# Scaled triangle rows of a state-space loop: sixteen GpSimd products against sixty-four ScalarE copies

## The chip, the cores and the metric

One core of a Trainium2 chip runs the whole program. Times are device microseconds (us) of an execution; the kernel before has a median of 1226.52 us over three runs (1224.99 to 1226.83). The trace belongs to one further execution, which took 1224.43 us, with a span of 1222.6 us from its first to its last instruction.

## The reference, cut to what matters

The network has two layers over 256 latent and 256 context tokens. The second one mixes attention with a state-space scan, run forwards and backwards over chunks of 128 tokens. Inside one chunk the scan needs, for each of 16 heads, a 128 x 128 matrix of decays:

```python
acs = jnp.cumsum(a.reshape(b, nc, Q, G, hg), axis=2)          # a = dt * A, Q = 128
lower = jnp.tril(jnp.ones((Q, Q), dtype=bool))[:, :, None, None]
seg = acs[:, :, :, None] - acs[:, :, None, :]
decay = jnp.exp(jnp.where(lower, seg, -jnp.inf))
cb = jnp.einsum('bcign,bcjgn->bcijg', Cm, Bm)
y = jnp.einsum('bcijgh,bcjghp->bcighp', cb[..., None] * decay, xdt)
...
y = y + jnp.einsum('bcign,bcghpn->bcighp', Cm, h_in) * jnp.exp(acs)[..., None]
```

The kernel gets seg from a matrix product. A triangle of ones (`before` or `after`) is multiplied with another triangle (`upto` or `from`) whose row k is scaled by a of token k. The scaled triangle is called rx. Its values for one head are 128 x 128; four heads lie beside each other in one slot of 128 x 512.

## The kernel before, in words

The program is written engine by engine, each engine with its own instruction stream, and semaphores order them. Nothing is scheduled automatically: an engine runs its instructions in written order and stops at the first wait that is not met.

Most of the time is matrix products of three parts each on TensorE (lines 1795 to 1797). Between the second layer's input projection and its attention stands the state-space stage, about 848 to 907 us in the trace. It ends in a loop of eight rounds k = 0 to 7 (`SEG`): four groups of four heads, two chunks each. A round has, in both directions d:

- **rx** (line 629, GpSimd): the scaled triangles of round k, two products of 128 x 512, in two of four slots. The slots of round k come free when the decay products of round k - 2 have read them (`seg_mm`).
- **decays(k)** (line 2266, TensorE): both directions' triangle products, summed in one of three PSUM banks `RB`. Each takes 128x512 of rx. Issued three rounds ahead: decays(k + 3) stands between the two other products of round k.
- **exp(k)** (line 968, ScalarE): the exponential of that bank, into `seg`.
- **mask products** (line 1605, VectorE): seg times the C-B products `CB`, one per direction. Both of its inputs lie in SBUF.
- **carried-state factors** (line 1611, VectorE): `CD` times `Cc`. The `CD` rows are broadcast into SBUF by DMAs that ScalarE issues (`rows_out`, line 939).
- **intra(k)** (line 2290, TensorE): the products within a chunk. **inter(k)** (line 2300, TensorE): the products with the carried state.
- Every second round also has `gate_y` on VectorE (lines 1594, 1596), `square_y` on ScalarE (line 959) and `sum_y` on TensorE (line 2274).

TensorE's order in round k is intra(k), decays(k + 3), inter(k), and then perhaps sum_y. ScalarE's order from round 1 to 5 is exp(k), a wait for inter(k - 1), two DMA issues, perhaps square_y, exp(k + 1). That wait is `act.wait_ge(s("inter_mm"), k)`.

Ahead of the loop VectorE scales the rows `XW` (line 1465), TensorE forms the chunk states from them (line 2256), ScalarE copies four of these out of PSUM (line 950), and VectorE joins them (1566, 1570).

Of the kernel before, what the change touches and what calls it, by code (L numbers as in the profile page):

```python
# [22 lines left out]
ALU = mybir.AluOpType  # L23
ACT = mybir.ActivationFunctionType
AX = mybir.AxisListType

P = 128
# [130 lines left out]
def build_trunk(nc, a, out):  # L158
    with ExitStack() as ctx:
        def sem(name):  # L160
            return ctx.enter_context(nc.semaphore(name))
# [16 lines left out]
        def view(name, shape, offset, dtype=F32):  # L178
            return nc.alloc_sbuf_tensor_at(name, [P] + list(shape), dtype, offset=offset)
# [72 lines left out]
        dts = view("dts", [8, TT * 32], r_misc + 24576)  # L252
# [38 lines left out]
        def cst(name, lo=0, hi=None, p0=0, p1=P):  # L291
            s, n = CONST_COLS[name]
            return const[p0:p1, s + lo:s + (n if hi is None else hi)]
# [14 lines left out]
        def s(name):  # L308
            if name not in S:
                S[name] = sem(name)  # L310
            return S[name]

        raw_loaded = [s(f"raw_loaded{i}") for i in range(RAW_SLOTS)]
        hi_split, lo_split, block_done = s("hi_split"), s("lo_split"), s("block_done")
# [23 lines left out]
        for n, (_, src, col) in enumerate(blocksA):  # L338
            stream.append(("w", src, 0, KD, col, BC))
            if 1 <= n <= 8:  # L340
                stream.append(("mod", 0, 1, n - 1))
# [33 lines left out]
        C_OUT = NW()  # L375
# [9 lines left out]
        rx = view("rx", [4, 512], r_split + idle)  # L385
# [37 lines left out]
        def _(sp):  # L423
# [15 lines left out]
            def load(r):  # L439
                item = stream[r]  # L440
                free(r)
                if item[0] == "mod":
                    _, l, j, k = item
                    if (l, j) == (1, 2):
                        rows_, cols_ = 2 * P * (k % 4), j * MOD_COLS + D * (k // 4)
                        sp.dma_start(raw_block(r, 2, D), tiles(a["mod_w"][l, rows_:rows_ + 2 * P, cols_:cols_ + D]))\
                            .then_inc(raw_loaded[r % RAW_SLOTS], 16)
                        return
                    sp.dma_start(raw[:, r % RAW_SLOTS, :],
                                 a["mod_w"][l, k * P:(k + 1) * P, j * MOD_COLS:(j + 1) * MOD_COLS])\  # L450
                        .then_inc(raw_loaded[r % RAW_SLOTS], 16)
                else:
                    _, src, k0, kt, col, cols = item
                    sp.dma_start(raw_block(r, kt, cols), src[:, k0:k0 + kt, col:col + cols])\
                        .then_inc(raw_loaded[r % RAW_SLOTS], 16)
# [146 lines left out]
        @block.gpsimd  # L602
        def _(pool):
            step = Chain(pool, s("pool_step"))

            nc.gpsimd.memset(U[:, :, :, :], 0.0).then_inc(s("pads_A"), 1)

            for f in range(KD):
                if f % 2:

                    pool.wait_ge(s("h_lo_dve"), f // 2 + 1)
                    nc.gpsimd.memset(ptap[:, f:f + 1], 0.0).then_inc(s("h_lo"), 1)
                    continue
                pool.wait_ge(s("h_hi"), f + 1)
                nc.gpsimd.tensor_tensor(Hlo[:, f, :], n_h[:, f % 4, :], Hhi[:, f, :].bitcast(F32), ALU.subtract)\  # L615
                    .then_inc(s("h_lo"), 1)

            pool.wait_ge(s("h_lo"), 3 * KD)
            nc.gpsimd.memset(XB[:, :, :, 0:2], 0.0).then_inc(s("pads_C"), 1)
            nc.gpsimd.memset(XB[:, :, :, 2 + LAT:4 + LAT], 0.0).then_inc(s("pads_C"), 1)  # L620
            pool.wait_ge(s("pads_C"), 2)
            pool.wait_ge(block_done, C_OUT)
            pool.wait_ge(s("da_ready"), 1)
            for k, (b, c) in enumerate(SEG):
                if k >= 2:
                    pool.wait_ge(s("seg_mm"), k - 1)
                for d in range(2):
                    at_ = 32 * c + 16 * d + 4 * b
                    nc.gpsimd.tensor_tensor(rx[:, (2 * k + d) % 4, :].rearrange("p (h i) -> p h i", h=4),
                                            cst(("upto", "from")[d]).unsqueeze(1).to_broadcast([P, 4, P]),  # L630
                                            dts[:, 7, at_:at_ + 4].unsqueeze(2).to_broadcast([P, 4, P]), ALU.mult)\
                        .then_inc(s("rx_ready"), 1)


        @block.scalar
        def _(act):
            step = Chain(act, s("act_step"))
            split = splitters(act, "hi")
            A = nc.scalar.activation
# [57 lines left out]
            for n, (kind, _, _) in enumerate(blocksA):  # L697
# [6 lines left out]
                if kind in ("k", "q"):  # L704
# [3 lines left out]
                    if nk == 0:  # L708
# [4 lines left out]
                      scale=vec[:, g0:g0 + 1]).then_inc(read_act, 1)  # L713
# [152 lines left out]
            for n, (kind, _, _) in enumerate(blocksC):  # L866
# [21 lines left out]
                if kind == "x":  # L888
# [3 lines left out]
                    if j < 5:  # L892
                        for i in range(2):
                            ins = A(XB[:, 2 * j + i, :, 2:2 + LAT], acc[:, lo + i, :].rearrange("p (s t) -> p s t", s=2),
                                    ACT.Copy)
# [40 lines left out]
            def rows_out(q):  # L936

                (b, c), d = SEG[q // 2], q % 2
                act.dma_start(CD[q % 6], row_store[2 * c + d, 4 * b:4 * b + 4, :].rearrange("h i -> (h i)")
                              .partition_broadcast(P)).then_inc(s(f"cd_loaded{q % 6}"), 16)  # L940

            act.wait_ge(s("qsc_copied"), 1)
            A(qsc[:, 0:LT, :], qsc[:, 0:LT, :], ACT.Sqrt, scale=1.0 / C_HD, bias=epsc[:, 0:1]).then_inc(s("qsc_root"), 1)
            act.wait_ge(s("row_stored"), 32)
            act.wait_ge(s("cb_mm"), 1)
            rows_out(0)
            rows_out(1)
            for k in range(4):
                act.wait_ge(s("xw_used"), (2, 2, 5, 5)[k])
                A(state[:, k // 2 * 2, k % 2, :], stbank[k // 2 * 4 + k % 2], ACT.Copy).then_inc(s("state_act"), 1)  # L950
            act.wait_ge(s("xw_used"), 6)

            def square_y(b):

                for f in (2 * b, 2 * b + 1):
                    act.wait_ge(s("yg_ready"), f + 1)
                    if f >= 2:
                        act.wait_ge(s("ssy_mm"), f - 1)
                    A(ysq[:, f % 2, :], XC[:, f, 0:LAT], ACT.Square).then_inc(s("ysq_ready"), 1)


            for q in range(2, 6):
                rows_out(q)
            for k in range(8):
                act.wait_ge(s("seg_mm"), k + 1)
                if k >= 2:
                    act.wait_ge(s("intra_mm"), k - 1)
                A(seg[:, (2 * k + 1) % 4, :], RB[k % 3][:, :], ACT.Exp).then_inc(s("decay_ready"), 1)
                if 1 <= k < 6:
                    act.wait_ge(s("inter_mm"), k)  # L970
                    for q in (2 * k + 4, 2 * k + 5):
                        rows_out(q)
                if k % 2 == 1 and k > 1:
                    square_y(k // 2 - 1)
# [1398 lines left out]
SEG = [(b, c) for b in range(4) for c in range(2)]  # L2373
# [58 lines left out]
```

## Time and profile before

| what | value |
|---|---|
| median of three runs | 1226.52 us (1224.99 to 1226.83) |
| the profiled execution, and its span | 1224.43 us, 1222.6 us |
| TensorE busy | 1163.7 us, 95% |
| VectorE busy | 715.9 us, 59% |
| ScalarE busy | 483.2 us, 40% |
| GpSimd busy | 30.2 us, 2%, 31 instructions |
| the chain that ended last | TensorE 77%, VectorE 17%, DMA 2%, ScalarE 2% |

The shares say that TensorE sets the time nearly everywhere. They are a mean over stages, so the state-space stage has to be read by itself: in the profile's 40 slices of 30.6 us, TensorE's digit is under 9 in the first two, in the last, and in the 29th and 30th (856 to 917 us), where the state-space loop runs. GpSimd's digit is 5 in the 29th slice, 1 in the 28th, 2 in the second, and 0 in all others.

### The profile page before, as it was taken

The numbers are of one execution on the slowest core, as the hardware profiler recorded it, in microseconds if no ns is written. First come the engines' busy times: TensorE is split into PE (matmuls) and PEld (weight loads), VectorE is DVE, ScalarE is ACT, GpSimd is POOL, SyncE is SP. The second block draws the span as 40 slices with busy tenths as digits, with TensorE's granted clock in tenths as the row PEclk, the third lists the DMA queues.
The fourth block names the chain that finished last, engine by engine and source line by source line (L and its number), as shares of the span: only waits on it lengthen the run. The fifth ranks groups of instructions, "written<-read, shape, count | busy, mean of one in ns | idle before, by whom it ended". The sixth has DMA issues, their size and how long they took to land.

```text
span 1222.6 us, 18071 instructions
## 1 busy us (share of the span) xinstructions
PE 1163.7 (95%) x7366; PEld 943.9 (77%) x7366; DVE 715.9 (59%) x1167; ACT 483.2 (40%) x720; POOL 30.2 (2%) x31
## 2 busy tenths in 40 slices
PE   4799999999999999999999999999889999999998
PEld 2477775677678888888887668898455798999998
DVE  2779997843543333423333378977979645556544
ACT  3413325652443332222222333464148735554432
POOL 0200000000000000000000000001500000000000
PEclk9799999999999999999999999999999999999999
DMA  8745436016553223333124553434214157646632
GB/s 323 285 138 175 161 138 215 2 61 214 174 172 103 86 58 98 126 115 103 57 67 151 191 192 109 131 115 147 84 37 139 36 173 254 194 132 215 203 111 96
DMA packets 123308, 170.70 MB, mean 140 GB/s; under 512 B 4797, under 2 KB 112743, under 8 KB 117991
## 3 DMA queue, kind: packets, MB, share of 16 engines
q1 hardware_dynamic: 120406, 164.99, 40.6%
q10 hardware_dynamic: 2833, 4.74, 1.2%
q8 instruction: 50, 0.82, 0.3%
q14 instruction: 19, 0.16, 0.0%
HBM read 168.63 MB, written 1.08 MB: 139 GB/s over the span
## 4 chain that ended last, share of the span: by engine, by line
PE 77%; DVE 17%; DMA 2%; ACT 2%; issue 2%; SPq 0%; POOL 0%; ACTq 0%; DVEq 0%
PE acc L1795 21%; PE acc L1796 20%; PE acc L1797 20%; DVE Y L1174 5%; PE pmod L1740 2%; DVE w_lo L544 2%; PE acc L1812 1%; PE acc L1814 1%; PE acc L1813 1%; PE p L1701 1%; PE acc L1701 1%; PE p L2347 1%; DVE seg L1605 1%; PE acc L2321 1%; DMA raw<-in_mod_w 1%
## 5 line engine op out<-in xcount | busy, mean ns | idle before, releaser
L544 DVE TENSOR_TENSOR w_lo<-raw,w_hi 128x1024 fp32r<-128x1024 f32 x234 | 259.6, 1151 | 242.0 <-ACT w_hi L535 241.7
L535 ACT ACTIVATE w_hi<-raw 128x1024 fp32r<-128x1024 f32 (+1 forms) x236 | 221.6, 987 | 438.4 <-PE acc L1797 408.0
L1795 PE MATMUL acc<-Hhi,w_hi 128*128 128x512 f32 (+1 forms) x992 | 339.7, 342 | 8.1 <-POOL Hlo L615 5.8
L1797 PE MATMUL acc<-Hhi,w_lo 128*128 128x512 f32 (+1 forms) x992 | 337.3, 340 | 0.0
L1796 PE MATMUL acc<-Hlo,w_hi 128*128 128x512 f32 (+1 forms) x992 | 337.2, 340 | 0.0
L1795 PEld LDWEIGHTS acc<-Hhi,w_hi 128*128 128x128 f32 x992 | 188.5, 190 | 33.6 <-issue 10.0
L1797 PEld LDWEIGHTS acc<-Hhi,w_lo 128*128 128x128 f32 x992 | 188.4, 190 | 20.9
L1796 PEld LDWEIGHTS acc<-Hlo,w_hi 128*128 128x128 f32 x992 | 188.6, 190 | 20.5
L1795 PE MATMUL acc<-hid_hi,w_hi 128*128 128x512 f32 (+1 forms) x448 | 157.1, 351 | 0.0
L1796 PE MATMUL acc<-hid_lo,w_hi 128*128 128x512 f32 (+1 forms) x448 | 155.7, 348 | 0.0
L1797 PE MATMUL acc<-hid_hi,w_lo 128*128 128x512 f32 (+1 forms) x448 | 155.7, 348 | 0.0
L1795 PEld LDWEIGHTS acc<-hid_hi,w_hi 128*128 128x128 f32 x448 | 84.8, 189 | 15.2 <-issue 4.8
L1797 PEld LDWEIGHTS acc<-hid_hi,w_lo 128*128 128x128 f32 x448 | 84.8, 189 | 10.8
L1796 PEld LDWEIGHTS acc<-hid_lo,w_hi 128*128 128x128 f32 x448 | 84.8, 189 | 10.3
L1174 DVE SCALAR_TENSOR_TENSOR Y<-U,vec,Y 128x512 f32<-128x512 f32 x120 | 82.4, 746 | 0.2
L1369 DVE TENSOR_TENSOR f_h<-acc,f_gate 128x1024 f32<-128x1024 f32 (+1 forms) x22 | 21.1, 958 | 103.1 <-PE acc L1797 100.5
L1335 DVE SCALAR_TENSOR_TENSOR X<-acc,mod,X 128x256 f32<-128x256 f32 (+1 forms) x72 | 30.6, 478 | 53.9 <-PE acc L1797 53.9
L1740 PE MATMUL pmod<-raw,cvec 128*32 128x512 f32 x320 | 43.7, 629 | 4.2 <-DMA raw<-in_mod_w 4.2
L1812 PE MATMUL acc<-Hhi,w_hi 128*128 128x512 f32 (+1 forms) x96 | 35.4, 369 | 2.4 <-DVE Hlo L1118 2.4
L1795 PE MATMUL acc<-mixC_hi,w_hi 128*128 128x256 f32 x128 | 36.6, 286 | 0.0
L1796 PE MATMUL acc<-mixC_lo,w_hi 128*128 128x256 f32 x128 | 36.2, 283 | 0.0
L1797 PE MATMUL acc<-mixC_hi,w_lo 128*128 128x256 f32 x128 | 36.2, 283 | 0.0
(298 smaller groups left out, 1333.7 us busy)
## 6 DMA issues: line engine op xcount, KB each, us to landing
raw<-in_mod_w SPq DMA_DIRECT2D x48, 1024.0 KB, 5.1
raw<-in_ffn_w_in SPq DMA_DIRECT2D x44, 1024.0 KB, 5.1
raw<-in_od_w_in SPq DMA_DIRECT2D x15, 1024.0 KB, 5.3
raw<-in_ffn_w_out SPq DMA_DIRECT2D x16, 768.0 KB, 4.5
raw<-in_ev_w_in SPq DMA_DIRECT2D x10, 1024.0 KB, 7.6
raw<-in_ffn_w_out SPq DMA_DIRECT2D x16, 640.0 KB, 4.3
raw<-in_od_w_out SPq DMA_DIRECT2D x8, 1024.0 KB, 5.1
raw<-in_ev_w_out SPq DMA_DIRECT2D x8, 768.0 KB, 5.9
```

Of the source, the lines that this page charges most:

```text
L535: nc.scalar.activation(w_hi[:, w % 2, c0:c1], raw[:, r % RAW_SLOTS, c0:c1], ACT.Copy)\
L544: nc.vector.tensor_tensor(w_lo[:, w % 2, c0:c1], raw[:, r % RAW_SLOTS, c0:c1], w_hi[:, w % 2, c0:c1].bitcast(F32), ALU.subtract).then_inc( ...
L1174: ins = V_.scalar_tensor_tensor(out=y, in0=U[:, i, :, tap:tap + LAT], scalar=col, in1=y, op0=ALU.mult, op1=ALU.add)
L1335: ins = V_.scalar_tensor_tensor(out=xs, in0=acc[:, 2 * pair + i, cols], scalar=gt, in1=xs, op0=ALU.mult, op1=ALU.add)
L1369: V_.tensor_tensor(f_h[:, :, 0:t], acc[:, 2:4, 0:t], f_gate[:, :, 0:t], ALU.mult)\
L1605: V_.tensor_tensor(heads4(seg[:, (2 * k + d) % 4, :]), both_ways, CB[:, 4 * d + 2 * c + b // 2, :].unsqueeze(1).to_broadcast([P, 4, P]), A ...
L1701: return nc.tensor.transpose(o, x, cst("ident", 0, n, 0, n))
L1740: ins = mm(pmod[32 * g:32 * g + 32, :], cvec[:, k, :], raw[:, r % RAW_SLOTS, g * 512:(g + 1) * 512], start=(k == 0), stop=(k == KD - 1))
L1795: mm(outs[m], hi[:, j, cols], xh, start=(first and j == 0), stop=False)
L1796: mm(outs[m], hi[:, j, cols], xl, start=False, stop=False)
L1797: ins = mm(outs[m], lo[:, j, cols], xh, start=False, stop=(last and j == kts - 1))
L1812: mm(o, hi[:, j, cols], xh, start=(j == 0), stop=False)
```

## The change

GpSimd no longer builds rx. ScalarE builds it, as a Copy with a scale that is read per partition from SBUF: each slot of 128x512 takes four instructions of 128 x 128, one per head. Sixteen GpSimd instructions become sixty-four on ScalarE. The slots and their waits are as before, and `rx_ready` still counts one per slot. The new function `step_rows(k)` is called for round 0 after the first two DMA issues, for round 1 after two of the four state copies, for round 2 after the other DMA issues and ahead of the loop, and for rounds 3 to 7 directly after exp(1) to exp(5).

```diff
-            pool.wait_ge(block_done, C_OUT)
-            pool.wait_ge(s("da_ready"), 1)
-            for k, (b, c) in enumerate(SEG):
-                if k >= 2:
-                    pool.wait_ge(s("seg_mm"), k - 1)
-                for d in range(2):
-                    at_ = 32 * c + 16 * d + 4 * b
-                    nc.gpsimd.tensor_tensor(rx[:, (2 * k + d) % 4, :].rearrange("p (h i) -> p h i", h=4),
-                                            cst(("upto", "from")[d]).unsqueeze(1).to_broadcast([P, 4, P]),
-                                            dts[:, 7, at_:at_ + 4].unsqueeze(2).to_broadcast([P, 4, P]), ALU.mult)\
-                        .then_inc(s("rx_ready"), 1)
...
+            def step_rows(k):
+
+                b, c = SEG[k]
+                if k >= 2:
+                    act.wait_ge(s("seg_mm"), k - 1)
+                for d in range(2):
+                    for h in range(4):
+                        col = 32 * c + 16 * d + 4 * b + h
+                        ins = A(rx[:, (2 * k + d) % 4, h * P:(h + 1) * P], cst(("upto", "from")[d]), ACT.Copy,
+                                scale=dts[:, 7, col:col + 1])
+                    ins.then_inc(s("rx_ready"), 1)
+
             act.wait_ge(s("row_stored"), 32)
             act.wait_ge(s("cb_mm"), 1)
             rows_out(0)
             rows_out(1)
+            act.wait_ge(s("da_ready"), 1)
+            step_rows(0)
             for k in range(4):
                 act.wait_ge(s("xw_used"), (2, 2, 5, 5)[k])
                 A(state[:, k // 2 * 2, k % 2, :], stbank[k // 2 * 4 + k % 2], ACT.Copy).then_inc(s("state_act"), 1)
+                if k == 1:
+                    step_rows(1)
             act.wait_ge(s("xw_used"), 6)
...
             for q in range(2, 6):
                 rows_out(q)
+            step_rows(2)
             for k in range(8):
                 act.wait_ge(s("seg_mm"), k + 1)
                 if k >= 2:
                     act.wait_ge(s("intra_mm"), k - 1)
                 A(seg[:, (2 * k + 1) % 4, :], RB[k % 3][:, :], ACT.Exp).then_inc(s("decay_ready"), 1)
+                if k + 2 < 8 and k:
+                    step_rows(k + 2)
                 if 1 <= k < 6:
                     act.wait_ge(s("inter_mm"), k)
                     for q in (2 * k + 4, 2 * k + 5):
```

The order of ScalarE's instructions changes at two places. The first is the way into the loop: the DMA rows are `rows_out`, `state<-` are the state copies, `seg<-p` is the exponential. In the kernel before:

```order
L939 DMA XC<-row_store 128x512 [waits cb_mm,row_stored]
L939 DMA XC<-row_store 128x512
L950 ACTIVATE state<-acc 128x512 [waits xw_used] x2
L950 ACTIVATE state<-p 128x512 [waits xw_used] x2
L939 DMA Cd<-row_store 128x512 [waits xw_used]
L939 DMA Cd<-row_store 128x512 x3
L968 ACT_TABLE_LOAD
L968 ACTIVATE seg<-p 128x512 [waits seg_mm] x2
```

In the changed kernel, whose line numbers are 12 lower here at first and then higher:

```order
L927 DMA XC<-row_store 128x512 [waits cb_mm,row_stored]
L927 DMA XC<-row_store 128x512
L940 ACTIVATE rx<-const,dts 128x128 [waits da_ready]
L940 ACTIVATE rx<-const,dts 128x128 x7
L952 ACTIVATE state<-acc 128x512 [waits xw_used] x2
L940 ACTIVATE rx<-const,dts 128x128 x8
L952 ACTIVATE state<-p 128x512 [waits xw_used] x2
L927 DMA Cd<-row_store 128x512 [waits xw_used]
L927 DMA Cd<-row_store 128x512 x3
L940 ACTIVATE rx<-const,dts 128x128 [waits seg_mm]
L940 ACTIVATE rx<-const,dts 128x128 x7
L973 ACT_TABLE_LOAD
```

Three sets of eight rx copies stand there, and the third stands in front of the table load and the first exponential.

The second place is the loop itself, ScalarE in rounds 1 to 3. In the kernel before:

```order
L939 DMA XC<-row_store 128x512 [waits inter_mm]
L939 DMA XC<-row_store 128x512
L968 ACTIVATE seg<-p 128x512 [waits intra_mm,seg_mm]
L939 DMA Cd<-row_store 128x512 [waits inter_mm]
L939 DMA Cd<-row_store 128x512
L968 ACTIVATE seg<-p 128x512 [waits intra_mm,seg_mm]
L939 DMA Cd<-row_store 128x512 [waits inter_mm]
```

In the changed kernel:

```order
L973 ACTIVATE seg<-p 128x512 [waits seg_mm] x2
L940 ACTIVATE rx<-const,dts 128x128 [waits seg_mm]
L940 ACTIVATE rx<-const,dts 128x128 x7
L927 DMA XC<-row_store 128x512 [waits inter_mm]
L927 DMA XC<-row_store 128x512
L973 ACTIVATE seg<-p 128x512 [waits intra_mm,seg_mm]
L940 ACTIVATE rx<-const,dts 128x128 [waits seg_mm]
L940 ACTIVATE rx<-const,dts 128x128 x7
L927 DMA Cd<-row_store 128x512 [waits inter_mm]
```

Each exponential from the second on is now followed by eight rx copies, and the next wait for `inter_mm` stands behind them. TensorE's and VectorE's instructions stand in the same order as before.

## Rows read from the trace of the kernel before

**Rows 1.** Stretches: length, busy of PE, PEld, DVE, ACT, POOL; granted clock, DMA share, GB/s.
```profile
873.30:892.76 19.46, 17.19 (x152) 10.50 (x154) 19.15 (x28) 3.00 (x6) 7.35 (x6) 1.00 0.35 109
892.76:900.60 7.84, 5.36 (x68) 3.80 (x64) 4.92 (x10) 2.66 (x7) 0.00 (x0) 1.00 0.20 67
...
899.00:901.00 2.00, 0.35 (x8) 0.35 (x8) 1.93 (x5) 1.36 (x3) 0.00 (x0) 1.00 0.00 0
901.00:904.00 3.00, 2.97 (x30) 2.50 (x26) 1.53 (x3) 0.95 (x2) 0.00 (x0) 0.52 0.00 0
```

**Rows 2.** The chain that ended last, in the loop: start, us, what.
```profile
872.49 1.46 DVE seg L1605
...
884.10 0.66 PE acc L2290 x8
```

**Rows 3.** ScalarE's timeline in the loop: start, us, engine, line [idle before].
```profile
852.54 1.09 ACT L950 ACTIVATE state<-acc 128x512 f32<-128x512 f32 x2 [2.93 <-PE acc L2256]
859.22 1.08 ACT L950 ACTIVATE state<-p 128x512 f32<-128x512 f32 x2 [5.59 <-PE p L2256]
...
864.62 1.28 ACT L968 ACT_TABLE_LOAD   x1 [4.31 <-issue]
865.91 1.09 ACT L968 ACTIVATE seg<-p 128x512 f32<-128x512 f32 x2
873.30 0.33 ACTq L939 DMA_DIRECT2D XC<-row_store  x1
...
874.21 0.60 ACT L968 ACTIVATE seg<-p 128x512 f32<-128x512 f32 x1 [7.21 <-PE acc L2300]
...
883.75 0.72 ACT L959 ACTIVATE ysq<-XC 128x256 f32<-128x256 f32 x2 [3.16 <-PE acc L2300]
884.38 0.58 ACT L968 ACTIVATE seg<-p 128x512 f32<-128x512 f32 x1
...
892.76 0.33 ACTq L939 DMA_DIRECT2D Cd<-row_store  x1
```

**Rows 4.** TensorE's timeline of round 2, and one later inter.
```profile
878.87 1.04 PE L2290 MATMUL acc<-seg,HF 128*64 128x128 f32 x16
879.84 1.98 PE L2266 MATMUL p<-rx,const 128*128 128x512 f32 x4
881.75 1.09 PE L2300 MATMUL acc<-Cd,state 128*64 128x128 f32 x16
...
902.29 1.92 PE L2300 MATMUL acc<-Cd,state 128*64 128x128 f32 x16
```

**Rows 5.** VectorE's groups from 866.6 to 903 us.
```profile
L1605 DVE TENSOR_TENSOR seg<-seg,X 128x512 f32<-128x512 f32 x16 | 14.8, 924 | 3.1 <-ACT seg L968 2.8
L1611 DVE TENSOR_TENSOR Cd<-Cd,Cc 128x512 f32<-128x512 f32 x10 | 7.3, 768 | 0.0
L1611 DVE TENSOR_TENSOR XC<-XC,Cc 128x512 f32<-128x512 f32 x6 | 6.4, 1102 | 0.0
```

**Rows 6.** VectorE's timeline: single instructions.
```profile
850.92 1.68 DVE L1465 TENSOR_TENSOR XW<-HF,DW 128x1024 f32<-128x1024 f32 x1 [0.93 <-PE acc L2256]
853.66 1.21 DVE L1465 TENSOR_TENSOR XW<-HF,DW 128x1024 f32<-128x1024 f32 x1
896.40 0.69 DVE L1605 TENSOR_TENSOR seg<-seg,X 128x512 f32<-128x512 f32 x1
```

**Rows 7.** GpSimd's timeline: the first four products together, then single ones.
```profile
847.49 4.04 POOL L629 TENSOR_TENSOR rx<-const,dts 128x512 f32<-128x512 f32 x4 [129.84 <-PE acc L1797]
...
869.02 1.48 POOL L629 TENSOR_TENSOR rx<-const,dts 128x512 f32<-128x512 f32 x1
```

**Rows 8.** ScalarE's timeline elsewhere: small shapes, and a scale or bias from SBUF.
```profile
120.55 1.27 ACT L719 ACTIVATE krt<-p,epsc 128x512 f32<-128x512 f32 x2 [0.30 <-PE p L1853]
...
702.76 1.70 ACT L686 ACTIVATE Hhi<-n_h,mod 128x256 fp32r<-128x256 f32 x4 [1.25 <-DVE n_h L1109]
725.17 0.50 ACT L535 ACTIVATE w_hi<-raw 128x128 fp32r<-128x128 f32 x2
```

## The prediction

> **What bounds the kernel now.** The table of engine shares puts TensorE at 95% of the span, so a microsecond lost in front of a TensorE product in any stage is a microsecond of the time, as long as nothing later takes it up; behind this stage TensorE runs on products whose weights are loaded ahead, so I let a delay pass through unchanged. The second view is the chain that ended last, within the loop. It runs on VectorE's mask products first (a wait of TensorE for line 1605), and from 884.10 on TensorE itself, [rows 2]. The third view is busy time by stretch. From 873.30 to 892.76 VectorE is busy 19.15 of 19.46 us, TensorE 17.19, ScalarE only 3.00 and GpSimd 7.35 [rows 1]. So two engines are nearly full and ScalarE has 16 us free: by shares the move looks harmless. Those two times are moments when ScalarE starts the DMA issues behind inter(0) and behind inter(4) [rows 3]; between them lie four periods of the loop, 4.87 us each on the mean.
>
> The fourth view is single instructions, and it shows what GpSimd costs. A mask product takes 0.69 us with GpSimd at rest [rows 6]. The sixteen of them took 14.8 us, and the sixteen products of line 1611, of the same shape, 7.3 + 6.4 us [rows 5]. With 32 x 0.69 = 22.1 us that is 6.4 us too much, all while GpSimd worked. GpSimd's own products, 4.04 us for four at first, take 1.48 us in the loop [rows 7]. One XW product of line 1465 at 850.92 took 1.68 us and the next 1.21 us, also beside GpSimd: 0.47 us on the way into the loop [rows 6].
>
> **Removed.** The sixteen GpSimd products go, and with them those 6.4 us of VectorE. Little of it is worth anything by itself: from 884.10 on TensorE is the chain's engine, and the ends of the DVE work only count where TensorE waits for line 1605. I credit the 0.47 us ahead of the loop in full, and in the loop nothing, because there something else is now later than VectorE (below).
>
> The Trainium skill, "SBUF — State Buffer", section "SBUF: two separate sides", describes the pair of SBUF ports that VectorE and GpSimd share as an exclusive lock, in which the loser waits for a whole instruction. The trace agrees (0.69 us becomes 1.4 to 1.5). Read alone, that rule would make the change a gain; what it would be worth is the third rival.
>
> **Added: sixty-four copies.** The length of a copy of 128x128 with its scale in SBUF isn't in the trace, so it is bounded. From below: two 128x128 copies without a pointer took 0.50 us together; at about 0.30 us for one they start 0.20 apart [rows 8]. From above: the same 0.30 us plus the pointer's 0.09, with no overlap: 0.39 apart. What a pointer adds to the distance of two starts: the krt pair, which has one, took 1.27 us for two, the exponentials at 865.91 without one 1.09 for two of 0.60, so 0.49 apart [rows 3, 8]; half of the difference, 0.18 / 2 = 0.09 us, is the pointer. Four SBUF copies of 128x256 with a pointer took 1.70 us, one being 0.50 long, so 0.40 apart [rows 8]; two of 128x256 without one took 0.72 together, about 0.31 apart, and again 0.09 less [rows 3]. 0.20 + 0.09 = 0.29 us is the value I take, with 0.38 us from a copy's start to its end. Eight then take 7 x 0.29 + 0.38 = 2.41 us until the second slot is ready, and hold ScalarE for 8 x 0.29 = 2.32 us.
>
> The Trainium skill, "ScalarE: Activation LUTs", section "What ACT_TABLE_LOAD costs", gives 186 ns plus 0.833 ns per element, 93 ns for each pointer operand, and an overlap of 93 ns between neighbours. For 128 elements that is an estimate of 0.386 us, 0.293 apart, so 2.44 us for eight: the fixed part is paid four times for a slot. The rows above agree, and by the rule my sum would be 0.1 to 0.2 us higher.
>
> **The way into the loop.** Rounds 0 and 1 are hidden: ScalarE idles 2.93 us in front of the first two state copies and 5.59 us in front of the next two [rows 3], and eight copies of 2.32 us fit into each; without that cover they would cost up to 2.3 us each. Round 2 is not hidden. Its copies stand ahead of the table load and of exp(0), at 864.62 in the old trace [rows 3], 864.15 with the 0.47 us gained. The load then starts at 864.15 + 2.32 = 866.47, exp(0) 1.29 later at 867.76 (it was 865.91), exp(1) at 868.25, the copies of round 3 at 868.74, ready at 871.15. VectorE starts its first mask product at 868.4 and no longer at 866.7, but both are done by 869.8 since each takes 0.7 us and not 1.5; intra(0) is over at 870.4. TensorE then needs decays(3), whose second half waits for the copies, 0.1 us for the semaphore, 0.96 us for that half (1.91 / 2, from the start of decays to the start of inter, [rows 4]), and 1.14 us from inter's start to ScalarE's next DMA issue (1.09 of product [rows 4], 0.05 to see it). That gives 873.35, with the semaphores 873.45: 0.15 us later than 873.30. The late exponential and the faster VectorE nearly cancel.
>
> **The periods.** Now the loop closes on ScalarE. Behind its wait for inter(k - 1) stand, in this order, the two DMA issues, exp(k + 1) and the copies for decays(k + 3), which TensorE must have before inter(k). The period is 0.91 (DMA issues, 873.30 to 874.21) + 0.49 (exponential) [rows 3] + 2.41 (eight copies) + 0.10 + 0.96 + 1.14 = 6.01 us. Four of these and one square_y (883.75 to 884.38, 0.63 us [rows 3]) are 24.67 us in place of 19.46: +5.21 us. TensorE meanwhile finishes intra(k) about 1 us after inter(k - 1) and then stands still for 1.7 us. VectorE, with 0.7 us products, is done earlier than before everywhere. The DMAs of `rows_out` are issued each 1.2 us later per period, but they are for three rounds on and are not waited for. From inter(4) on no copies are left (round 7's lie ahead of that moment), so the tail of the stage keeps its length.
>
> **The sum.** +0.15 + 5.21 = +5.4 us. Against the profiled execution: 1224.43 + 5.4 = 1229.8 us. That execution lies 2.1 us under the median of the runs, so the median should be 1226.52 + 5.4 = 1231.9 us. With copies 0.20 us apart: eight take 1.70 us, the period is 5.30 us, 21.8 us for the four, +2.4; ahead of it TensorE and no longer the copies sets inter(0), 0.5 us earlier; +1.9 in all, 1228.4 us. With 0.39: eight take 3.12 us, the period 6.72 us, +8.1, and 1.5 ahead of the loop; +9.6, 1236.1 us.
>
> **Rivals.** (1) *TensorE's clock falls.* The new loop leaves TensorE idle for some 2 of 6 us in each period. The granted clock was 1.00 in all of the old loop, busy 17.19 of 19.46 us, and 1.00 where TensorE was busy 5.36 of 7.84 us; but after 899 to 901 us, where TensorE was busy 0.35 us of 2, it fell to 0.52 for 3 us, which is the 1.2 GHz level for nearly all of it [rows 1]. At that level inter took 1.92 us and not 1.09 [rows 4]. The half of decays and the inter of each period would cost some 0.9 + 0.8 = 1.7 us more. For two to four periods: +3.4 to +6.8 on top, 1235.3 to 1238.7 us. Against it: the shares of the new loop are like those of 892.76 to 900.60, where it didn't fall. Chance 0.15, price 1237.
>
> (2) *The pointer costs nothing when copies stand back to back*, and the lower bound holds: 1228.4 us, or a little less where the copies begin sooner than I let them. The krt pair speaks against it. Chance 0.12.
>
> (3) *Faster: VectorE was the true limit, and the copies run in ScalarE's idle time.* ScalarE has 16 us free and the eight copies need 2.3 us of a period of 4.87. If TensorE never waited for rx, the loop would fall to TensorE's own work, 0.97 + 1.91 + 0.93 = 3.81 us of round from the starts in [rows 4], four times, plus 1.06 for one sum_y: 16.3 us and not 19.46, and the median 1226.52 - 3.2 = 1223.3 us. What decides is where the copies stand: they follow exp(k + 1), and that follows the wait for inter(k - 1). Of a period of (19.46 - 0.63) / 4 = 4.71 us, 3.60 are taken by the other steps of the cycle, so eight copies would have to be done in 1.11 us to break even, 0.12 us apart. Even the lower bound is above that. It comes true only if I have the cycle wrong, for example if ScalarE issues its DMAs beside its copies. Chance 0.07.
>
> **Chances.** The forecast, +3 to +9.6 us with its place at +5.4: 0.66; clock 0.15; free pointer 0.12; faster 0.07. Slower by over 0.2% (2.5 us, about what a measurement of this kernel can tell from no change) is 0.66 + 0.15 = 0.81; within 0.2% lies the free pointer with its +1.9 us: 0.12; faster: 0.07. The range from 1227.6 to 1237.6 takes in both bounds of the copy and half of the clock's case, and leaves out the faster case and the clock's worst.
>
> **What would show it.** Right: the copies of 128x128 last about 0.38 us and stand 0.29 apart; VectorE's mask products are all at 0.69 us; TensorE's idle time in front of decays (line 2266 or its weight load) is put down to ScalarE, about 1.7 us four times; the moments at which ScalarE starts the paired DMA issues are 6.0 us apart; the first exponential starts some 1.9 us later than before. Wrong: periods of about 4 us (rival 3), or an idle TensorE in front of line 2290 with VectorE as its releaser, or a granted clock near 0.5 within the loop (rival 1); or a copy of 0.30 us, 0.20 apart (rival 2).

## The result and the profile after

The changed kernel takes 1235.06 us, the median of four runs (1232.95 to 1235.23), against 1226.67 us for the kernel before in the same measurement (four runs, 1224.99 to 1227.83). The ratio is 1.0068, with a 95% interval from 1.0055 to 1.0081: 8.4 us slower, 6.7 to 9.9 by the interval.

The profiled executions differ by more, 1233.5 against 1222.6 us of span. Of these 10.9 us, 2.3 lie ahead of the state-space stage: its first DMA issue (line 939, now 927) starts at 851.08 and not at 848.76 us. Ahead of it nothing was changed but GpSimd's first products, which began at 847.49 [rows 7]; and e9_gpsimd_late, which has the instructions of the kernel before up to there, issues at 850.89, so this moment moves by itself between executions. What follows is therefore counted from that issue. From there to the attention's first scores (line 2321, now 2328) it was 907.18 - 848.76 = 58.42 us before, and is 917.77 - 851.08 = 66.69 us: +8.3 us, close to the difference of the medians (8.4).

VectorE's groups in the stage of the changed kernel, to set beside [rows 5]:

```profile
L1612 DVE TENSOR_TENSOR seg<-seg,X 128x512 f32<-128x512 f32 x16 | 11.0, 689 | 16.8 <-ACT seg L973 16.6
L1618 DVE TENSOR_TENSOR Cd<-Cd,Cc 128x512 f32<-128x512 f32 x10 | 6.4, 683 | 0.0
L1618 DVE TENSOR_TENSOR XC<-XC,Cc 128x512 f32<-128x512 f32 x6 | 3.9, 683 | 0.0
```

The thirty-two products now all take 0.69 us; 7.2 us of busy time are gone (6.4 in the prediction, which set overlapped busy times against lengths that don't overlap). But VectorE now waits 16.6 us for exponentials. The gain was turned into idle time.

ScalarE's timeline, from the way into the loop to the fifth paired DMA issue (start, us, engine, line), to set beside [rows 3]:

```profile
864.66 1.78 ACTq L927 DMA_DIRECT2D Cd<-row_store  x4
866.49 2.44 ACT L940 ACTIVATE rx<-const,dts 128x128 f32<-128x128 f32 x8 [4.32 <-PE p L2273]
868.95 1.28 ACT L973 ACT_TABLE_LOAD   x1
870.25 1.08 ACT L973 ACTIVATE seg<-p 128x512 f32<-128x512 f32 x2
871.22 2.44 ACT L940 ACTIVATE rx<-const,dts 128x128 f32<-128x128 f32 x8
877.70 0.81 ACTq L927 DMA_DIRECT2D XC<-row_store  x2
878.62 0.60 ACT L973 ACTIVATE seg<-p 128x512 f32<-128x512 f32 x1 [4.96 <-PE acc L2297]
879.11 2.43 ACT L940 ACTIVATE rx<-const,dts 128x128 f32<-128x128 f32 x8
883.79 0.81 ACTq L927 DMA_DIRECT2D Cd<-row_store  x2
...
891.27 0.81 ACTq L927 DMA_DIRECT2D Cd<-row_store  x2
...
897.92 0.81 ACTq L927 DMA_DIRECT2D XC<-row_store  x2
...
904.00 1.89 ACTq L927 DMA_DIRECT2D Cd<-row_store  x2
```

Eight copies take 2.44 us everywhere. The moments of the paired issues give periods of 6.09, 7.48, 6.65 and 6.08 us, 26.30 in all where it was 19.46.

TensorE's timeline of the same stretch (as in [rows 4]):

```profile
871.78 1.29 PE L2297 MATMUL acc<-seg,HF 128*64 128x128 f32 x16 [1.67 <-DVE seg L1612]
873.00 3.37 PE L2273 MATMUL p<-rx,const 128*128 128x512 f32 x4
876.31 1.35 PE L2307 MATMUL acc<-XC,state 128*64 128x128 f32 x16
877.49 1.04 PE L2297 MATMUL acc<-seg,HF 128*64 128x128 f32 x16
880.52 2.20 PE L2273 MATMUL p<-rx,const 128*128 128x512 f32 x4 [1.99 <-ACT rx L940]
882.65 1.09 PE L2307 MATMUL acc<-Cd,state 128*64 128x128 f32 x16
883.58 1.04 PE L2297 MATMUL acc<-seg,HF 128*64 128x128 f32 x16
886.61 3.27 PE L2273 MATMUL p<-rx,const 128*128 128x512 f32 x4 [1.99 <-ACT rx L940]
889.80 1.42 PE L2307 MATMUL acc<-Cd,state 128*64 128x128 f32 x16
...
894.65 2.20 PE L2273 MATMUL p<-rx,const 128*128 128x512 f32 x4 [2.55 <-ACT rx L940]
```

In front of three of the loop's five decays TensorE waits 2 to 2.6 us for the copies (line 940), and in front of the last one 0.77 us. And two of the five last 3.3 to 3.4 us in place of 2 to 2.2: the granted clock fell twice. Busy time by stretch (columns as in [rows 1]):

```profile
870.00:872.00 2.00, 0.33 (x5) 0.25 (x6) 1.02 (x2) 1.99 (x6) 0.00 (x0) 1.00 0.10 39
873.00:876.00 3.00, 3.00 (x6) 0.91 (x4) 2.97 (x5) 0.66 (x3) 0.00 (x0) 0.57 0.00 0
...
887.00:890.50 3.50, 3.50 (x10) 1.31 (x10) 1.11 (x2) 0.63 (x3) 0.00 (x0) 0.51 0.12 39
```

### The profile page after: what moved, and what is told of

The parts are those of the page before. It is cut to its first block, busy times and chain, and to the rows that moved or that the text cites. A ratio compares the mean times of both kernels' runs of the same rounds, so it can differ in the third digit from the quotient of the medians.

```text
span 1233.5 us, 18119 instructions
## 1 busy us (share of the span) xinstructions
PE 1169.2 (95%) x7366; PEld 945.8 (77%) x7366; DVE 707.4 (57%) x1167; ACT 501.9 (41%) x784; POOL 10.5 (1%) x15
## 4 chain that ended last, share of the span: by engine, by line
PE 78%; DVE 14%; ACT 3%; DMA 2%; issue 2%; ACTq 0%; SPq 0%; POOL 0%; DVEq 0%
PE acc L1802 21%; PE acc L1804 20%; PE acc L1803 20%; DVE Y L1181 4%; PE pmod L1747 2%; PE p L1708 1%; DVE w_lo L544 1%; PE acc L1819 1%; PE acc L2328 1%; PE p L2273 1%; PE acc L1708 1%; PE acc L1820 1%; PE acc L1821 1%; PE p L2354 1%; DMA raw<-in_ffn_w_in 1%
```

## The experiments

All nine kernels were measured with five rounds against the kernel before, in three groups. Each line of this table compares within its group; the stage is the distance defined above, in the profiled execution. That is one execution, and not always a middle one: e2_fill's is the longest of its five (1232.82 us), e8_both's the shortest (1214.81) and e1_ahead's 1.4 us under its median.

| kernel | median us | before in its group | ratio (95%) | stage us |
|---|---|---|---|---|
| the changed kernel | 1235.06 | 1226.67 | 1.0068 (1.0055 to 1.0081) | 66.69 |
| e2_fill | 1230.60 | 1225.67 | 1.0038 (1.0025 to 1.0051) | 63.29 |
| e3_wide | 1227.99 | 1225.67 | 1.0021 (1.0009 to 1.0033) | 58.93 |
| before | | | 1 | 58.42 |
| e1_ahead | 1222.83 | 1225.67 | 0.9974 (0.9964 to 0.9984) | 55.53 |
| e9_gpsimd_late | 1222.31 | 1225.59 | 0.9972 (0.9961 to 0.9983) | 54.54 |
| e7_tail | 1220.73 | 1225.39 | 0.9958 (0.9945 to 0.9972) | 53.73 |
| e5_mixed | 1220.29 | 1225.39 | 0.9956 (0.9942 to 0.9970) | 53.06 |
| e4_memset | 1219.65 | 1225.67 | 0.9959 (0.9945 to 0.9972) | 52.36 |
| e6_late_issue | 1219.47 | 1225.39 | 0.9955 (0.9942 to 0.9969) | 51.19 |
| e8_both | 1217.27 | 1225.59 | 0.9931 (0.9917 to 0.9944) | 48.92 |

### e1_ahead: the same copies, one round earlier

```diff
-                if k + 2 < 8 and k:
-                    step_rows(k + 2)
+                if k + 3 < 8:
+                    step_rows(k + 3)
```

> All sixty-four copies stay on ScalarE; the eight of round k + 3 are now made after exp(k), one round earlier than in the changed kernel, so they no longer stand between the wait for inter(k - 1) and the decays that need them at once. Theory A (the cost is the place of the copies in ScalarE's order, a cycle of DMA issues, exponential, copies, half of decays, inter): TensorE no longer waits for rx, the four periods between the paired DMA issues fall from 26.3 us to about 17 (TensorE's own work; ScalarE's is 0.91 + 0.49 + 2.35 + 0.3 = 4.05 us a period), VectorE's products stay at 0.69 us, and the median is about 1224 us, under the kernel before. Rival B (the cost is ScalarE's extra work, 19 us of short instructions, wherever they stand): the median stays at 1234 to 1236 us.

Measured 1222.83 us, ratio 0.9974. TensorE's timeline from round 0 on:

```profile
869.41 1.29 PE L2297 MATMUL acc<-seg,HF 128*64 128x128 f32 x16 [1.67 <-DVE seg L1612]
870.63 1.98 PE L2273 MATMUL p<-rx,const 128*128 128x512 f32 x4
872.54 1.09 PE L2307 MATMUL acc<-XC,state 128*64 128x128 f32 x16
873.47 1.04 PE L2297 MATMUL acc<-seg,HF 128*64 128x128 f32 x16
874.44 1.98 PE L2273 MATMUL p<-rx,const 128*128 128x512 f32 x4
```

No idle time stands in front of any decays; a round takes 3.81 us of TensorE's own work (872.54 to 876.35 for two starts of inter). The four periods are 890.14 - 873.68 = 16.5 us. All sixty-four copies are still there, at 2.44 us for eight. Rival B is out: in the loop the amount of ScalarE's work cost nothing, its place did. (What the eight copies ahead of the loop cost is asked in e5_mixed.)

### e2_fill: idle time of TensorE filled

```diff
+            def fill(n):
+
+                for _ in range(n):
+                    mm(pmod[:, LAT:2 * LAT], cst("ones"), cst("cosA"), start=False, stop=True, skip_group_check=True)
+
+            fill(3)
...
                 if k + 3 < 8:
+                    fill((0, 3, 3, 3, 1)[k])
                     decays(k + 3)
```

> The changed kernel with thirteen added TensorE products of 128x256 into an unused half of a PSUM bank, in the stretches in which TensorE stands idle: three ahead of the loop's first intra, and 3, 3, 3 and 1 ahead of decays in rounds 1 to 4. Nothing reads them. Theory A adds that the two stretches at half clock (873 to 876 and 887 to 890.5 us) cost 1.4 to 1.7 us each: with the idle time filled the granted clock stays at 1.00 in the loop and the median falls by 2.5 to 3.5 us, to about 1232. Rival C (the low clock lies beside ScalarE's copies and costs nothing): the clock may stay up, the median stays within 0.7 us of 1235. If the fillers were in the way of decays the time would rise.

Measured 1230.60 us, ratio 1.0038 where the changed kernel had 1.0068; the two intervals just miss each other (1.0051 and 1.0055); in the medians +4.9 us stand against +8.4. The row of the four periods, beside the same of the changed kernel:

```profile
876.96:901.87 24.91, 22.72 (x172) 13.41 (x170) 13.65 (x25) 12.32 (x38) 0.00 (x0) 1.00 0.30 86
```

```profile
877.70:904.00 26.30, 19.00 (x152) 10.58 (x150) 13.59 (x24) 12.32 (x38) 0.00 (x0) 0.94 0.28 80
```

The granted clock is 1.00 in the four periods, as it is ahead of them, and the periods are 6.09, 6.09, 6.64 and 6.09 us. So in the loop this is the cycle alone, without the clock. (In the tail, which has no fillers, it fell in this execution.) The fall of the clock was a cost of its own, as the theory had it: 1.6 us ahead of the periods and 1.4 us in them.

### e3_wide: two wide copies a round in place of eight

```diff
-                    for h in range(4):
-                        col = 32 * c + 16 * d + 4 * b + h
-                        ins = A(rx[:, (2 * k + d) % 4, h * P:(h + 1) * P], cst(("upto", "from")[d]), ACT.Copy,
-                                scale=dts[:, 7, col:col + 1])
+                    col = 32 * c + 16 * d + 4 * b
+                    ins = A(rx[:, (2 * k + d) % 4, :].rearrange("p (h i) -> p h i", h=4),
+                            cst(("upto", "from")[d]).unsqueeze(1).to_broadcast([P, 4, P]), ACT.Copy,
+                            scale=dts[:, 7, col:col + 1])
```

> The changed kernel with one copy of 128x512 per slot in place of four of 128x128: all four heads get the first head's scale, so this leaves out the other three scales. Eight copies of 2.44 us per round become two, about 0.71 us long and 0.62 apart, 1.33 us until the second slot is ready. Theory A: each period gets 1.1 us shorter, and so does the way into the loop; 6.09 becomes 5.0 us, the clock falls less often or not at all, and the median is 1227 to 1229.5 us. Rival C (only the clock's falls made the change slower): the periods stay near 6 us and the median at 1232 or above.

Measured 1227.99 us, ratio 1.0021. ScalarE's and TensorE's timelines of one period:

```profile
876.50 1.32 ACT L939 ACTIVATE rx<-const,dts 128x512 f32<-128x512 f32 x2
880.38 0.81 ACTq L927 DMA_DIRECT2D Cd<-row_store  x2
```

```profile
877.35 1.96 PE L2273 MATMUL p<-rx,const 128*128 128x512 f32 x4 [1.44 <-ACT rx L939]
879.24 1.09 PE L2307 MATMUL acc<-Cd,state 128*64 128x128 f32 x16
```

The time came out as expected, the period did not quite: 5.29 us (880.38 to 885.67) and not 5.0. The second copy is ready while the first half of decays still runs, so the whole of decays (1.89) lies behind the first copy (0.71), in place of its second half (0.96) behind both (1.33). That adds 0.3 us. The slope is the cycle's: less time in the copies, less time in the period. Rival C, clock alone, is out. The twelve times of this kernel fall apart into seven from 1224.95 to 1228.39 us, with a mean granted clock of 0.990 to 0.994, and five from 1230.00 to 1231.51 us, with 0.988 or 0.989: the same program meets a falling clock more in some executions than in others.

### e4_memset: GpSimd writes and doesn't read

```diff
-                    nc.gpsimd.tensor_tensor(rx[:, (2 * k + d) % 4, :].rearrange("p (h i) -> p h i", h=4),
-                                            cst(("upto", "from")[d]).unsqueeze(1).to_broadcast([P, 4, P]),
-                                            dts[:, 7, at_:at_ + 4].unsqueeze(2).to_broadcast([P, 4, P]), ALU.mult)\
+                    nc.gpsimd.memset(rx[:, (2 * k + d) % 4, :], 0.0)\
```

> The kernel before, with GpSimd writing zeros to rx in place of the products: it leaves out the scaled triangles and reads no SBUF, at the same places and with the same waits. It measures what VectorE's contention with GpSimd cost. Theory A: every line 1605 and 1611 product takes 0.69 us, the loop falls to TensorE's own work, about 17 us for the four periods in place of 19.46 and 2 us less ahead of inter(0), and the median is 1222 to 1223.5 us. Rival D (a GpSimd instruction holds the shared port whether it reads or not, or TensorE was the limit all along): products stay at 1.4 us, or they shrink and the median stays within 0.7 us of 1226.7.

Measured 1219.65 us, ratio 0.9959: 6.0 us faster in the medians and 6.06 in the stage, more than the 3 to 4.5 expected. VectorE and GpSimd in the loop:

```profile
L1603 DVE TENSOR_TENSOR seg<-seg,X 128x512 f32<-128x512 f32 x16 | 11.0, 690 | 6.5 <-ACT seg L966 6.2
```

```profile
866.07 0.99 POOL L629 MEMSET rx<- 128x512 f32 x2 [0.73 <-PE p L2264]
867.79 0.99 POOL L629 MEMSET rx<- 128x512 f32 x2 [0.73 <-PE p L2264]
```

GpSimd's writes fall among VectorE's products and slow none of them. The four periods are 888.19 - 871.74 = 16.45 us. This is what contention cost the kernel before: 3 us in the periods (19.46 to 16.45) and 1.8 us ahead of them. The remaining 1.2 us of the stage lie in the tail, where the clock fell before and doesn't this time, and are not shown to be contention. A write is also shorter than a product (0.5 us for 1.0 or more), but TensorE never waited for rx in the kernel before, so that is no rival. The change removed the contention in full; the gain was there to be had.

### e5_mixed: round 2 back on GpSimd

```diff
+            pool.wait_ge(s("seg_mm"), 1)
+            for d in range(2):
+                at_ = 32 * SEG[2][1] + 16 * d + 4 * SEG[2][0]
+                nc.gpsimd.tensor_tensor(rx[:, d, :].rearrange("p (h i) -> p h i", h=4),
...
+                    .then_inc(s("rx_pool"), 1)
...
-            step_rows(2)
```

> e1_ahead with the two slots of round 2 built by GpSimd as before (rounds 0, 1 and 3 to 7 on ScalarE). Theory A: what is left of the change's cost ahead of the loop is round 2, whose eight copies stand in front of the table load and exp(0). exp(0) starts 1.9 us to 2.4 us earlier, VectorE has no product in the first 1.5 us of GpSimd's two, and intra(0) follows the three decays with no more than 0.3 us of idle time in place of 1.67. The median falls by 1.5 to 2 us from e1_ahead, to about 1221. Rival: TensorE is held there by the decays themselves, or GpSimd takes back what exp(0) gains: within 0.7 us of 1222.8.

Measured 1220.29 us, ratio 0.9956. The first exponential follows the DMA issues and the table load, and TensorE has no idle time ahead of intra(0):

```profile
864.70 5.31 PE L2284 MATMUL p<-rx,const 128*128 128x512 f32 x12
869.94 1.09 PE L2308 MATMUL acc<-seg,HF 128*64 128x128 f32 x16
```

The stage is 2.5 us shorter than in e1_ahead and the median 2.5 us lower. The intervals of the two ratios overlap, so the trace has to carry it: from the stage's start to the first paired issue it is 874.02 - 851.31 = 22.71 us, in e1_ahead 873.68 - 848.70 = 24.98, and the four periods are equal (16.46). So the way into the loop does cost something, as was supposed: the eight copies of round 2 in front of exp(0).

### e6_late_issue: the wait moved, the copies left

```diff
-                if 1 <= k < 6:
-                    act.wait_ge(s("inter_mm"), k)
-                    for q in (2 * k + 4, 2 * k + 5):
+                if 2 <= k < 7:
+                    act.wait_ge(s("inter_mm"), k - 1)
+                    for q in (2 * k + 2, 2 * k + 3):
                         rows_out(q)
```

> The changed kernel with the copies left where they are (after exp(k), for round k + 2) and the two DMA issues of a round, with their wait for inter, moved one round back, behind the copies. Theory A: the cycle is closed by that wait; with it moved, exp(k + 1) and the copies for round k + 3 start as soon as intra(k - 1) is done, TensorE no longer waits for rx in rounds 1 to 4, and the loop is as short as in e1_ahead: median 1222.5 to 1225. If the CD rows come too late VectorE waits for DMAs, in front of line 1618, and some of it is lost. Rival E (what counts is only how many rounds ahead the copies are made): decays still waits about 2 us for rx in each round and the median stays at 1232 to 1235.

Measured 1219.47 us, ratio 0.9955, better than the 1222.5 to 1225 expected. With the copies exactly where the change put them, TensorE is busy without a gap:

```profile
874.50:891.00 16.50, 16.50 (x154) 10.31 (x152) 14.18 (x27) 11.23 (x34) 0.00 (x0) 1.00 0.48 128
```

This settles which part of the cycle closes it: the wait for inter, with the issues behind it, standing in front of exp(k + 1) and the copies. Rival E (only the number of rounds matters) is out. No DMA came late. The part that wasn't foreseen is the tail: exp(6) no longer stands behind the last issues, and exp(7) behind a wait that is met a round earlier. TensorE starts the attention's scores 51.19 us after the stage's start, 4.3 us sooner than in e1_ahead, in whose trace the clock also fell in the tail.

### e7_tail: e1_ahead with exp(6) ahead of the last issues

```diff
             for k in range(8):
-                act.wait_ge(s("seg_mm"), k + 1)
...
+                if k != 6:
+                    decay_exp(k)
+                if k == 5:
+                    decay_exp(6)
```

> e1_ahead with exp(6) moved ahead of the last wait for inter, the last two DMA issues and square_y(1). In all kernels so far VectorE stands idle for about 3 us at the end of the loop until exp(6) comes from behind them. Theory A: VectorE's products of rounds 6 and 7 end earlier, intra(7) starts about 3 us earlier, its 1.65 us of idle time shrink, and the clock doesn't fall in the tail; median 1219 to 1220.5. Rival: the tail is held by sum_y and gate_y, and only 0.4 us is gained: 1222 to 1223.

Measured 1220.73 us, ratio 0.9958, 0.2 us above the expected range, and not told apart from e1_ahead by the intervals. The tail did get shorter, 903.45 - 892.89 = 10.56 us from the last pair of issues to the scores against 904.23 - 890.14 = 14.09, though part of that is e1_ahead's clock, which fell there. But in this execution the clock fell at the start of the loop, behind the idle time that e1_ahead has too:

```profile
870.51 1.29 PE L2304 MATMUL acc<-seg,HF 128*64 128x128 f32 x16 [1.67 <-DVE seg L1619]
871.74 3.45 PE L2280 MATMUL p<-rx,const 128*128 128x512 f32 x4
```

Up to here TensorE's timeline is the same in e1_ahead, e6_late_issue, e7_tail and the changed kernel, with the same gap of 1.67 us; behind it the clock fell in the last two and not in the first two. Confirmed in the trace, inconclusive in the time.

### e8_both: e6_late_issue and round 2 on GpSimd

> e6_late_issue (copies on ScalarE, the DMA issues and their wait behind them, one round back) with the two slots of round 2 built by GpSimd, as in e5_mixed. Theory A: the 1.67 us in front of intra(0) and the late issue are separate costs and add up: 1.3 to 2 us under e6_late_issue's 1219.5, about 1217.8. Rival: they share slack, and it stays within 0.6 us of 1219.5.

Measured 1217.27 us, ratio 0.9931 (0.9917 to 0.9944): 8.3 us under the kernel before and the lowest median of all. The stage is 48.92 us, 2.27 less than in e6_late_issue, the medians lie 2.2 us apart and the intervals just touch (0.9942 and 0.9944): as far as that goes, the two costs add up.

### e9_gpsimd_late: the kernel before with e6's order of issues

> The kernel before, GpSimd building all of rx, with only the DMA issues and their wait moved one round back, behind the next exponential. It tells how much of e6_late_issue's gain is the order of the issues and how much the move of the products. Theory A: the loop stays at VectorE's slowed pace up to round 3 (products of 1.4 us beside GpSimd), and only the tail gets shorter, since exp(6) and exp(7) no longer stand behind the last issues: 2 to 3 us, median about 1223. Rival: GpSimd's contention no longer matters once ScalarE's order is right, and the median comes to 1219 to 1220.5 as in e6_late_issue.

Measured 1222.31 us, ratio 0.9972, as theory A had it. The mask products are as slow as in [rows 5], the tail is shorter:

```profile
L1605 DVE TENSOR_TENSOR seg<-seg,X 128x512 f32<-128x512 f32 x16 | 14.8, 924 | 0.3
```

Between this kernel and e6_late_issue lies the change itself, in a good order: 1222.31 to 1219.47 us (0.9972 to 0.9955; in the stage 54.54 to 51.19). The same move of the products is worth +8.4 us behind the old order of ScalarE and -2 (by the ratios) to -3 us (by the stages) behind the new one. The intervals of the two ratios overlap, so that sign rests mainly on the stages.

## Why the prediction was right, step by step

It forecast slower, 1231.9 us in a range of 1227.6 to 1237.6, and measured were 1235.06. The number came 3 us above its place in the range, and those 3 us are nearly all the clock, which the forecast's likeliest case left out. It stayed in the range because the upper end had room for dearer copies and for half of the clock's case. The terms, each against the trace of the changed kernel and against e2_fill, where the clock stays up in the loop:

| term | forecast | changed kernel | e2_fill |
|---|---|---|---|
| to the first decays, without contention on XW | -0.47 | -0.46 | -0.46 |
| to ScalarE's issue behind inter(0), this included | +0.15 | +2.08 | +0.45 |
| four periods | +5.21 | +6.84 | +5.45 |
| tail to the scores | 0 | -0.65 | -1.03 |
| sum | +5.4 | +8.27 | +4.87 |

- **VectorE freed, and worth nothing in the loop.** Right: 0.69 us for each product, and it waits for ScalarE. The XW product took 1.22 us in place of 1.68. What was credited to the loop without contention, nothing, held only for this order of ScalarE; e4_memset shows 3 us in the four periods and 6.0 us in the medians.
- **A copy of 128x128 with a scale in SBUF.** 0.388 us long by the median, 2.44 us for eight, so 0.293 apart; forecast 0.38, 2.41 and 0.29. No row had this size with a scale from SBUF; the value came out of pairs of rows of other shapes.
- **The cycle.** The period was 6.09 us (877.70 to 883.79) where 6.01 was worked out. That the cycle is closed by ScalarE's wait is shown by e6_late_issue, that it is the place of the copies and not their number by e1_ahead, and that its length follows the copies by e3_wide.
- **The clock.** This is the term that was mis-sized. The likeliest case held the clock at 1.00 and gave the falling clock a chance of 0.15 as a rival. It did fall, twice, after 1.67 and after 1.99 us of idle TensorE. Set against e2_fill it cost 1.6 us ahead of inter(0) and 1.4 in the second period, 3.0 in all. (The stages differ by 3.4; the other 0.4 lie in the tail and are not the clock's, below.) The rival's price for one period, 1.7 us, was near enough for each fall. But it looked for falls in two to four periods, and one of the two came ahead of the first period, behind the late exponential, where it priced nothing. The argument used against it, that 892.76 to 900.60 had the same share of busy time at full clock [rows 1], overlooked how that stretch ends: with a gap of 1.65 us, behind which the clock did fall, in the row below. Nor does the length of a gap decide it: the longest of the new loop, 2.55 us, was followed by full clock.

```profile
900.66 1.85 PE L2290 MATMUL acc<-seg,HF 128*64 128x128 f32 x16 [1.65 <-DVE seg L1605]
```

- **The tail.** Forecast unchanged, measured 0.65 us shorter. Two things lie in it, and no run shows either to be an effect of the change. The first is luck of an execution: in the old trace the clock fell in it (0.52 from 901 to 904 us, [rows 1]); in the new one, behind a gap of 1.64 us, it didn't (1.00 from 904.00 to 917.77). Of the other traces that have this gap of 1.65 us, the clock fell in e1_ahead, e2_fill and e5_mixed, and not in e3_wide and e4_memset. The second thing is the last pair of DMA issues, behind which exp(6) stands: it took 1.57 us before, 1.89 in the changed kernel and only 0.81 in e2_fill, whose tail is the shortest of the three though its clock fell. Why that pair takes 0.8 to 1.9 us is open. The rows are, in this order, of the kernel before, the changed kernel and e2_fill:

```profile
892.76 1.57 ACTq L939 DMA_DIRECT2D Cd<-row_store  x2
```

```profile
904.00 1.89 ACTq L927 DMA_DIRECT2D Cd<-row_store  x2
```

```profile
901.87 0.81 ACTq L927 DMA_DIRECT2D Cd<-row_store  x2
```

The third rival's loop exists, too: four periods of 16.5 us, near the 16.3 worked out for it, but only once the copies or the wait are moved (e1_ahead, e6_late_issue).

## What to carry to other kernels

Before work is moved onto an engine because that engine is idle, follow what it waits for: here ScalarE was busy 3 of 19 us, but stood in a wait in front of the work that the critical engine needs next. What is put behind such a wait is added to the period as soon as the slack is used up: 2.44 us of copies made a period of 4.7 us one of 6.1. The cure is order, not speed: put what is needed soon ahead of the wait, or move the wait one round back. When a loop becomes bound by such a cycle, look also at what the idle gaps do to TensorE's clock, since that here cost 3 us on top of 5.

## What the runs showed of the hardware

- GpSimd slows VectorE's products of two SBUF inputs from 0.69 to 1.4 or 1.5 us only where GpSimd reads SBUF: as a writer of zeros (0.5 us for 128x512) it slowed none of them. The Trainium skill, "SBUF — State Buffer", section "SBUF: two separate sides", says the same of two-input operations, and here the trace agrees.
- The granted clock fell to the 1.2 GHz level after gaps of 1.67 us (changed kernel, e7_tail) and 1.99 us (changed kernel), and did not after equal or longer ones (1.67 us in e1_ahead and e6_late_issue; 1.99 us at 880.52 and 2.55 us at 894.65 in the changed kernel itself). Which gap is hit changes from one execution to the next, so one profile doesn't price it; filling the loop's gaps with thirteen useless products did: 3.0 us for two falls.
- A ScalarE copy whose input repeats a block of 128 four times through its access pattern took about 0.71 us for 128x512, two of them 1.33 together, so 0.62 apart, where four copies of 128x128 take 1.17. Between the two sizes that is (0.62 - 0.293) / 384 = 0.85 ns per element, so an estimated 0.11 us of the 0.293 for the elements and 0.18 us for each instruction whatever its size: the larger half of the change's work.
